# Gated rows of the experts turned in place, their buffer given up for a thirteenth slot of the weight ring

## The reference

```python
logits = (h @ w_router); top_v, top_i = lax.top_k(logits, 2)
gates = softmax(top_v)
for e in range(8):
    g, u = split(h @ w_gu[e], 2)          # w_gu[e]: 1024 x 7168
    out += combine[:, e:e+1] * ((silu(g) * u) @ w_down[e])   # w_down[e]: 3584 x 1024
return rmsnorm(h + out, ln_final)
```

## Time and profile before

| | |
|---|---|
| median of 3 runs | 1373.28 us (1373.19 to 1374.88) |
| the profiled execution | 1373.21 us, its span 1371.5 us |
| PE busy | 1308.7 us, 95% of the span |
| DVE, ACT, POOL busy | 35%, 26%, 3% |
| DMA | 445.11 MB, mean 325 GB/s |
| chain of waits | PE 74%, DMA 20%, DVE 3% |

### The profile page before, as it was taken

The page is one execution under the profiler, slowest core; times in us unless marked ns, Lnnn a source line. Parts: engine busy times, 40 slices in busy tenths (PEclk is TensorE's granted clock), DMA queues, the critical chain, the costliest instruction groups (busy, mean ns, idle before and its releaser), DMA issues.

```text
span 1371.5 us, 25177 instructions
## 1 busy us (share of the span) xinstructions
PE 1308.7 (95%) x11074; PEld 739.2 (54%) x11074; DVE 483.0 (35%) x740; ACT 361.1 (26%) x508; POOL 37.7 (3%) x62
## 2 busy tenths in 40 slices
PE   8999999999999999999999999999988999987885
PEld 7778888888899987443334333344332343332231
DVE  7775555446689984320111210120110120110112
ACT  6764444335578863200000100000000000000101
POOL 1000000000002221000000000000000000000000
PEclk9999999999999999999999999999999999999998
DMA  9345555555665646999999999999999999999994
GB/s 332 99 160 193 182 194 185 185 187 172 170 176 153 240 159 257 404 424 426 425 428 424 425 426 425 426 427 424 426 426 426 424 426 426 425 427 426 425 427 168
DMA packets 86221, 445.11 MB, mean 325 GB/s; under 512 B 7472, under 2 KB 33344, under 8 KB 62432
## 3 DMA queue, kind: packets, MB, share of 16 engines
q1 hardware_dynamic: 80688, 432.04, 79.0%
q10 hardware_dynamic: 5088, 10.75, 2.2%
q0 software_dynamic: 336, 0.71, 0.2%
HBM read 442.43 MB, written 1.05 MB: 323 GB/s over the span
## 4 chain that ended last, share of the span: by engine, by line
PE 74%; DMA 20%; DVE 3%; ACT 1%; DVEq 1%; issue 1%; SPq 0%; ACTq 0%
PE bank L1358 24%; PE bank L1376 12%; DMA e_ring<-moe_w_gu_in 12%; PE bank L851 10%; PE bank L853 10%; PE bank L852 10%; DMA e_ring<-moe_w_down_in 7%; PE bank L1326 1%; PE bank L1345 1%; DVE w_lo L1489 1%; DMA ring<-swa_w_qkv_in 1%; DVE acc L1825 1%; PE bank L1216 1%; ACT w_hi L558 1%; PE bank L1074 0%
## 5 line engine op out<-in xcount | busy, mean ns | idle before, releaser
L1358 PE MATMUL bank<-e_ring,xgT 128*32 128x512 f32 (+1 forms) x4864 | 467.8, 541 | 22.4 <-DMA e_ring<-moe_w_gu_in 21.1
L1358 PEld LDWEIGHTS bank<-e_ring,xgT 128*32 128x32 f32 x4864 | 155.3, 110 | 334.2 <-issue 294.4
L1376 PE MATMUL bank<-e_ring,m_hT 128*32 128x512 f32 (+1 forms) x2464 | 234.8, 538 | 18.3 <-DMA e_ring<-moe_w_down_in 18.3
L1489 DVE TENSOR_TENSOR w_lo<-ring,w_hi 128x2048 fp32r<-128x2048 f32 (+1 forms) x84 | 191.8, 2287 | 108.8 <-ACT w_hi L558 108.6
L558 ACT ACTIVATE w_hi<-ring 128x2048 fp32r<-128x2048 f32 (+1 forms) x84 | 158.9, 1895 | 127.9 <-PE bank L853 120.1
L1376 PEld LDWEIGHTS bank<-e_ring,m_hT 128*32 128x32 f32 x2464 | 78.5, 110 | 169.1 <-issue 126.6
L851 PE MATMUL bank<-w_hi,hT_hi 128*128 128x512 f32 (+1 forms) x336 | 130.8, 389 | 2.3 <-DVE w_lo L1489 1.9
L852 PE MATMUL bank<-w_lo,hT_hi 128*128 128x512 f32 (+1 forms) x336 | 129.1, 384 | 0.0
L853 PE MATMUL bank<-w_hi,hT_lo 128*128 128x512 f32 (+1 forms) x336 | 129.1, 384 | 0.0
L2059 DVE TENSOR_TENSOR m_sg<-m_sg,bank 128x512 f32<-128x512 f32 (+1 forms) x38 | 22.3, 613 | 229.3 <-PE bank L1358 229.3
L2073 DVE COPY m_sg<-bank 32x512 f32<-32x512 f32 (+1 forms) x22 | 13.4, 609 | 239.2 <-PE bank L1376 238.9
(11 more groups left out here) (350 smaller groups left out, 1215.7 us busy)
## 6 DMA issues: line engine op xcount, KB each, us to landing
e_ring<-moe_w_gu_in SPq DMA_DIRECT2D x128, 1792.0 KB, 33.9
e_ring<-moe_w_down_in SPq DMA_DIRECT2D x55, 2048.0 KB, 35.5
ring<-ffn_w_gu_in SPq DMA_DIRECT2D x28, 1024.0 KB, 5.2
ring<-ffn_w_down_in SPq DMA_DIRECT2D x14, 1024.0 KB, 4.9
ring<-ssm_w_in_in SPq DMA_DIRECT2D x8, 1024.0 KB, 5.1
ring<-ssm_w_in_in SPq DMA_DIRECT2D x16, 512.0 KB, 3.9
ring<-ssm_w_in_in SPq DMA_DIRECT2D x32, 256.0 KB, 4.6
ring<-ssm_w_out_in ACTq DMA_DIRECT2D x8, 1024.0 KB, 5.0
```

The costliest lines, as they stand in the source:

```text
L1358: ins = pe.matmul(hidden_bank(s, b)[quad_of(q)].rearrange("p (m v) -> p m v", v=STRIP), xgT[:, k, quad_of(b)], columns_of(e_slot(p * LAYER ...
L1376: ins = pe.matmul(bank[DOWN[b]][quad_of(q), 0:columns.stop - columns.start], m_hT[:, DOWN_ROWS * c + r, rows], wv[:, columns], start=(c == ...
L1489: dve.tensor_tensor(w_lo[:, m % RING, 0:w], ring[:, m % RING, 0:w], w_hi[:, m % SPLIT, 0:w].bitcast(F32), ALU.subtract).then_inc(lo_ready, 1)
```

## The change

- `m_hT` is given up. DVE turns the blocks of `m_sg` in place, and PE's `down` reads its weights from there (`hidden_T`); a weight load now takes 32 columns, each 16 bytes from the next.
- Several tables of the dense stages move: `jlt` and four small ones under `shares_T`, which becomes a tile of its own; `decay_of`, `sinks`, `dtb`, `alog`, `dsk` to a place below `HT_AT`, which the ring covers later. All tiles are aligned to 32 instead of 512 bytes.
- The ring begins 11776 bytes lower and has 13 places. For the tables under it, chunk 3 now waits for `c_stat` too.
- `final_gain` no longer lies in `m_sg`, but in the ring's place of the last up chunk of the last expert (`GAIN_OVER`); its DMA waits for that chunk to be used. SP waits for `gain_loaded` at the head of its loop, ahead of chunk 0, and ACT does no longer. ACT waits for `rows_ready` before its loop, since `ffn_gain` now lies under `m_sg`.

```diff
-FIRST_LAP = (2, 3, 4, 5, 6, 7, 8, 1, 9, 10, 11, 0)
+FIRST_LAP = (3, 4, 5, 6, 7, 8, 9, 2, 10, 11, 12, 0, 1)
 LANES = len(FIRST_LAP) + 1
-E_AT = 25600
+E_AT = 13824
+GAIN_OVER = 7 * LAYER_CHUNKS + GU_CHUNKS - 1
...
-        align = ALIGN if math.prod(shape[1:]) >= ALIGN // 4 else 32
-        return ctx.enter_context(nc.sbuf_tensor(name, shape, dt, align_bytes=align))
+        return ctx.enter_context(nc.sbuf_tensor(name, shape, dt, align_bytes=32))
...
-        jlt = sb("jlt", [P, E, E])
+        shares_all = sb("shares_T", [P, TT, P])
+        shares_T = shares_all[:, 0:TT]
+        jlt = shares_all[:, 0, 0:E * E].rearrange("p (e j) -> p e j", e=E)
+        rank_at, base_at, number, key_bias = (shares_all[:, 1, E * i:E * (i + 1)] for i in range(4))
...
+        decay_of, sinks_in, sinks, dtb, alog, dsk = phase(
+            HT_AT - 2048, decay_of=((3, P), F32), sinks_in=((HEADS,), F32), sinks=((HEADS,), F32), dtb=((SH,), F32),
+            alog=((SH,), F32), dsk=((SH,), F32))
...
-        m_sg, m_hT, xgT, shares_T = phase(
-            m_sg=((3 * sum(w for _, w in SETS),), F32), m_hT=((KT, CAP), F32), xgT=((KD, CAP), F32), shares_T=((TT, P), F32))
-        yg, final_gain = m_sg[:, 0:D], m_sg[:, D:2 * D]
+        m_sg, xgT = phase(m_sg=((3 * sum(w for _, w in SETS),), F32), xgT=((KD, CAP), F32))
+        yg, final_gain = m_sg[:, 0:D], e_ring[:, E_PLACE[GAIN_OVER]:E_PLACE[GAIN_OVER] + D]
...
+        def hidden_T(tile, b):
+
+            s = int(tile >= SETS[0][1] // QUAD)
+            m, r = divmod(tile - s * (SETS[0][1] // QUAD), DOWN_ROWS)
+            return hidden_rows(s, b).rearrange("p (m t r) -> p m r t", t=QUAD, r=DOWN_ROWS)[:, m, r]
...
                 sp.wait_ge(round_free, it + 1)
+                sp.wait_ge(gain_loaded, it * 16 + 16)
                 sp.wait_ge(c_dt_parts, 4)
                 for i in range(3):
                     expert_load(0, i)
                 sp.wait_ge(chunk_used, SO0)
+                sp.wait_ge(c_stat, G)
                 expert_load(0, 3)
...
             act.sem_inc(gain_loaded, 16)
+            act.wait_ge(rows_ready, TT)
             act.wait_ge(r_rounds, 1)
...
-                if p == 0:
-                    act.wait_ge(gain_loaded, it * 16 + 16)
...
                 if p == E - 1:
-                    act.wait_ge(m_T, it * (2 * E) + 2 * E)
+                    act.wait_ge(chunk_used, it * ROUND_CHUNKS + (MOE0 + GAIN_OVER + 1))
                     act.dma_start(final_gain, ln_final.partition_broadcast(P)).then_inc(gain_loaded, 16)
...
-                                                m_hT[:, DOWN_ROWS * c + r, rows], wv[:, columns],
+                                                hidden_T(DOWN_ROWS * c + r, rows), wv[:, columns],
...
-                        ins = dve.transpose(m_hT[:, tiles_of(s), quad_of(b)],
-                                            hidden_rows(s, b).rearrange("p (m i r) -> p m r i", i=QUAD, r=DOWN_ROWS))
+                        blocks = hidden_rows(s, b).rearrange("p (m i r) -> p m r i", i=QUAD, r=DOWN_ROWS)
+                        ins = dve.transpose(blocks, blocks)
```

More of the change, by code:

```diff
@@ L205, in build @@
         rt = sb("rt", [P, 16, TT * E])
+        acol = dts[:, 10:12].rearrange("p a b -> p (a b)")
+        root_table = sb("root_table", [P, 8])
         slot_row = dts[:, 0:8].rearrange("p (i a) b -> p i (a b)", i=2)
@@ L208, in build @@
         sel = rt[:, 0:12].rearrange("p (t a) b -> p t (a b)", t=TT)
-        acol = dts[:, 10:12].rearrange("p a b -> p (a b)")
-        root_table = sb("root_table", [P, 8])
-        decay_of = sb("decay_of", [P, 3, P])[:]
         choice = sb("choice", [P, 2, TT, E])
@@ L217, in build @@
         order_i = sb("order_i", [P, E + 1], I32)
[L218 to L221, removed]
         slot_at = sb("slot_at", [P, E])
@@ L273, in build @@
         dt_parts = acc[:, 0]
-        m_sg, m_hT, xgT, shares_T = phase(
-            m_sg=((3 * sum(w for _, w in SETS),), F32), m_hT=((KT, CAP), F32), xgT=((KD, CAP), F32), shares_T=((TT, P), F32))
-        yg, final_gain = m_sg[:, 0:D], m_sg[:, D:2 * D]
+        m_sg, xgT = phase(m_sg=((3 * sum(w for _, w in SETS),), F32), xgT=((KD, CAP), F32))
+        yg, final_gain = m_sg[:, 0:D], e_ring[:, E_PLACE[GAIN_OVER]:E_PLACE[GAIN_OVER] + D]
         raw_hT, = phase(raw_hT=((KD, T), F32))
-        ffn_gain, logits_T, cmp8, sel_first = phase(
-            3 * 4 * sum(w for _, w in SETS), ffn_gain=((D,), F32), logits_T=((T,), F32), cmp8=((2, TT, E * E), F32),
+        ffn_gain, _, logits_T, cmp8, sel_first = phase(
+            ffn_gain=((D,), F32), upper_raw_hT=((D,), F32), logits_T=((T,), F32), cmp8=((2, TT, E * E), F32),
             sel_first=((TT, SMALL), F32))
@@ L332, in down_at @@
             if b == 0:
-                return quad_of(q // 2), slice(q % 2 * 512, (q % 2 + 1) * 512)
-            return quad_of(2), slice(q * 256, (q + 1) * 256)
+                return q // 2, slice(q % 2 * 512, (q % 2 + 1) * 512)
+            return 2, slice(q * 256, (q + 1) * 256)
         def hidden_banks(p):
@@ L351, in columns_of @@
             return chunk[:, first:first + BLOCKS * w].rearrange("p (m q v) -> p q m v", q=BLOCKS, v=STRIP)[:, q]
-        def tiles_of(s):
-            return slice(SETS[s][0] // P, SETS[s][0] // P + BLOCKS * SETS[s][1] // P)
         def place_of(head):
@@ L831, in expert @@
                         rows_at, columns = down_at(b, q)
-                        act.activation(yg[rows_at, columns], bank[DOWN[b]][quad_of(q), 0:columns.stop - columns.start],
+                        act.activation(yg[quad_of(rows_at), columns], bank[DOWN[b]][quad_of(q), 0:columns.stop - columns.start],
                                        ACT.Copy).then_inc(y_act, 1)
@@ L2072, in expert @@
                         rows_at, columns = down_at(b, q)
-                        dve.tensor_copy(yg[rows_at, columns], bank[DOWN[b]][quad_of(q), 0:columns.stop - columns.start]
+                        dve.tensor_copy(yg[quad_of(rows_at), columns], bank[DOWN[b]][quad_of(q), 0:columns.stop - columns.start]
                                         ).then_inc(y_dve, 1)
```

## The result

The changed kernel takes 1419.05 us (median of 5 runs, 1418.75 to 1419.25), against 1373.28 for the kernel before (5 runs at the same place). The ratio is 1.0331, 95% interval 1.032 to 1.0343: 45.8 us slower. The profiled execution has a span of 1417.5 us, 46.0 more than before; some 0.7 us of that lie ahead of the experts: the first dense weights land 13.61 us after their issue (13.09 before), and the dense stages end 0.7 us later. This is variation between executions and not the change: ACT's copy of the logits, at the end of the dense stages, starts at 551.22 us before and at 551.89 now, but at 551.94 in experiment 5, which has the change and no loss.

The account below looks back on a forecast made before the run. The prediction took the DMA stream of expert weights, at 425 GB/s, as the bound. It added 45.7 us, between +46.1 by bytes and +45.4 by landings, and 0 for other parts, to 1373.2: 1418.9 us, range 1415 to 1426.

Parts of the forecast that it names:

- The two ways of adding up: Delay of the expert weight stream: by bytes +46.1 us, by landings of chunk 12 +45.4 us; 45.7 taken.
- the sum: Expert stream, by bytes: later start +13.7, eight chunks not carried early +34.5, ffn_gain -1.2, dips -0.9; together +46.1 us.
- What bounds the kernel: Expert stage: the DMA weight stream at 425 GB/s, 829 us in all, sets the last landing, not PE.
- The new wait: Head of SP's loop: chunk 0 waits for ACT's increment at 561.0 us, so the stream starts 13.7 us later.
- Not slower: Rival at SP's first lap: increment arrives before needed, deciding at about 499 us; 1372.7 us, chance 0.03.
- PE doesn't soften it: Expert stage: PE restarts near 568 us and waits for chunks in the first expert; lower clock absorbed; cost 0.
- The sign of being wrong: Expert stream traffic: a rate above 430 GB/s, or loads issued at 440 us, would refute the forecast.
- Thirteenth place: Ring's 13th slot: closes the dip at 566 us at the start, at most 0.5 us; buys nothing later.
- Turned rows and weight loads: In-place transposes and the down stage's strided weight loads: cost taken as 0; slow loads on top, chance 0.06.
- the bound of +6 us: Down stage: loads as slow as 128 contiguous columns move the end by about 6 us, to 1425; chance 0.06.
- the pace of 0.12 us: Down stage's slow-load case: one load per 0.12 us costs 2.7 us per small expert, 17.5 per large one.

Follow-up runs that it names:

- experiment 5: Changed kernel with ACT's first gain_loaded increment at program start and loads at most twelve chunks ahead despite 13 places; 1373.51 us, ratio 1.0003.
- experiment 3: Changed kernel with ACT's first gain_loaded increment right after its wait for the end of the dense stages; 1411.40 us, ratio 1.0282.
- run 8: Kernel before, with loads of experts 1 to 7 fetching only the left half of each chunk's columns (very last chunk whole); 1323.38 us, ratio 0.9635.
- run 9: Changed kernel with the gain_loaded increment at program start, loads of experts 1 to 7 fetching only half of each chunk (very last whole); 1323.87 us, ratio 0.9644.
- experiment 4: Changed kernel with ACT's first gain_loaded increment in its mixer loop, at 512.1 us; 1378.63 us, ratio 1.0039.
- experiment 2: Kernel before plus only the one line at the head of SP's loop that waits for gain_loaded; 1419.47 us, ratio 1.0337.
- experiment 1: Changed kernel with ACT's first gain_loaded increment moved to the start of its program, SP's wait kept; 1373.10 us, ratio 1.0003.
- experiment 7: Changed kernel with ACT's first gain_loaded increment ahead of the last dense loads, at 499.5 us; 1372.77 us, ratio 0.9999.
- experiment 6: Changed kernel with the gain_loaded increment at program start and the very last chunk loaded by one DMA instead of two halves; 1374.27 us, ratio 1.0011.

## Why the prediction was right

It said 1418.9 us, and 1419.05 was measured. That close is partly luck. The two ways of adding up gave 46.1 and 45.4 us, and 45.7 was picked between them; and of the 45.9 us by which the last landing on the chain moved, 0.7 came from ahead of the experts, which no step of the sum has.

- *What bounds the kernel.* That the stream of expert weights is the bound all the way through the experts, although the chain showed PE up to 968 us, is shown twice: by experiment 3, which moves it and leaves PE's start as it was, and by runs 8 and 9, where less to load makes the kernel 50 us faster. Experiment 4 moves both and does not part them. The bytes alone give the loss of every late run. The table sums what the DMA engines had carried by 610 us (windows of 5 us from 430 us on) and sets what is missing at 425 GB/s beside the delay of the last landing on the chain.

| run | MB by 610 us | missing | at 425 GB/s | last landing later |
|---|---|---|---|---|
| before | 50.8 | | | |
| changed | 31.1 | 19.7 | 46.3 us | 45.9 us |
| experiment 2 | 30.7 | 20.1 | 47.2 us | 46.8 us |
| experiment 3 | 34.8 | 16.1 | 37.8 us | 37.4 us |
| experiment 4 | 48.4 | 2.4 | 5.6 us | 5.5 us |

- *The new wait.* Its place, its release (561.0 predicted from the earlier trace rows, 561.6 in the changed kernel) and its price held; experiments 1 and 2 put the whole loss on this one line and its partner. The sum's working, start of the stream plus bytes no longer carried early, also gives experiment 3 to 0.9 us, within its interval, once the true time of the first load is put in.
- *Not slower, the rival, and its threshold.* The place was right: free at 499.5 us (experiment 7), 6 us at 512.1 (experiment 4). The reason I gave, idle time of the DMA engines that runs out, carries the larger part of these 6 us but not all. I had left out that late expert loads also delay the last dense weights, hence the end of the dense stages and the chunks that wait for it (1.7 us in experiment 4).
- *PE doesn't soften it.* Expert 0 goes at the DMA's pace, first matmul at 569.0 us (568 predicted), first Silu at 600.8 (600), last landing on the chain at 1396.3 (1396). The lower clock at PE's restart (0.50, until about 573 us) was taken up, as assumed: the first two chunks took 8.3 us where later ones take 3.2 each, and PE still waited 0.2 us for the third. Its waits for chunks 3 to 7 were 1.0 to 1.8 us a chunk (1.1 predicted). The sign of being wrong, a rate above 430 GB/s, did not show in windows of 20 us, as the earlier trace rows has them: from 565 to 1345 us they lie between 423 and 429. (Two windows of 5 us at the stream's start have 433.)
- *Thirteenth place: 0.5 us.* The medians of experiments 1 and 5 differ by 0.4, which is not to be told from zero.
- *Turned rows and weight loads: 0.* The transposes became 34 ns longer, not 1089. The weight loads became 28 ns longer (138 against 110), but keep the pace of 0.081 us in a large expert. So the bound of +6 us was not reached, and the pace of 0.12 us behind it did not come with PE as the bound either: it would have made run 9 66 us slower than run 8. What makes a load with this step 28 ns longer was not found; with loads that overlap, as these do, it stands on no path (690.9 us in run 8, 691.1 in run 9).

**What to carry to other kernels.** When a wait is moved to another engine, ask when the instruction that satisfies it is executed, not only that it comes some time: here an increment that was free for one engine stood 120 us too late for another. Where a transfer stream never rests, as here (423 to 429 GB/s from 565 to 1345 us), each microsecond of late start and each byte not carried early comes back in full at the end (46.3 us of missing bytes, 45.9 us of delay), however far the chain of waits runs over another engine. Sum the bytes up to a fixed time in both traces, and the loss can be read off halfway through the kernel. And where transfers share engines, a late release of prefetches can hurt the next transfers in line as well (landing after 15 and 24 us instead of 5 in experiment 4).

## What the runs showed of the hardware

- Weight loads of 32 columns with a step of 16 bytes between columns take 138 ns (changed kernel) instead of 110 (before), and matmuls of 256 columns still follow each other every 0.054 us (run 9: 36.29 us less 224 at 0.108, over 224).
- A transpose of 128x512 with a 16-byte step on both sides takes 1123 ns (changed kernel), with the step on the read side alone 1089 (before).
- At the end of the full stream the traffic falls from 425 to some 220 GB/s (mean of the changed kernel from 1388 to 1400 us), with the DMA engines' share near 0.5, for about 12 us before the stream ends, whether the last chunk is one DMA or two (experiment 6: 216 GB/s from 1342 to 1354 us). By estimate an even end would save some 5 us (2.7 MB at 425 GB/s take 6.3 us). What makes it uneven was not found.
- Two dense loads of 1 MB on ACT's queue, issued behind four expert chunks on SP's, landed after 15 and 24 us instead of 5 (experiment 4).
- PE's granted clock fell to 0.50 at a wait of about 1 us in some traces and stayed at 1.00 in others. In those of the kernel before and of run 8 it was at 0.50 from about 561.6 to 565 us, and the first 256 matmuls of expert 0 took 25.81 and 25.76 us; in experiments 1 and 9 it stayed at 1.00 and they took 24.26. In all four PE had waited 1.10 us just before. Near the end, behind a wait of 0.88 us, the eight matmuls ahead of the final norm took 3.68 us in experiment 1 and 4.93 in experiment 7, where the clock fell to 0.50 under them. The code of this part is the same in both, so medians that differ by about 1.5 us or less can mislead. What decides whether the clock falls was not found.
